# Start of a three-block kernel: the identity and the first norm's vector in transfers of their own, two weight slabs between the tiles of x, the first dense tile between the turns

## The reference, cut to what matters

```
h = rms_norm(x, attn_pre_g[l])          # x * rsqrt(mean(x*x) + eps) * g
proj = h @ w_in[l]                      # [512,1024] @ [1024,3080]
qa, ka, va, qb, kb, vb, f_logit = split(proj)
qa, ka = partial_rotary(qa, cos, sin), partial_rotary(ka, cos, sin)
lam = exp(sum(lam_q1*lam_k1)) - exp(sum(lam_q2*lam_k2)) + lam_init
log_f = log_sigmoid(f_logit + forget_bias[l])
```

## Time and profile before

| what | value |
|---|---|
| median of 3 runs | 2214.27 us (2210.42 to 2216.82) |
| profiled execution | 2209.98 us, its span 2208.7 us |
| PE busy | 2110.6 us, 96% of the span |
| DVE, ACT, POOL busy | 982.4, 814.2, 229.2 us |
| first slice of 40 (55 us): PE, DVE, ACT, POOL | 7, 6, 4, 2 tenths |
| DMA | 192.10 MB, mean 87 GB/s |

### The profile page before, as it was taken

The page is one execution under the profiler, slowest core; times in us unless marked ns, Lnnn a source line. Parts: engine busy times, 40 slices in busy tenths (PEclk is TensorE's granted clock), DMA queues, the critical chain, the costliest instruction groups (busy, mean ns, idle before and its releaser), DMA issues. The chain is left out here.

```text
span 2208.7 us, 25477 instructions
## 1 busy us (share of the span) xinstructions
PE 2110.6 (96%) x10364; PEld 1699.1 (77%) x10364; DVE 982.4 (44%) x1809; ACT 814.2 (37%) x1550; POOL 229.2 (10%) x263
## 2 busy tenths in 40 slices
PE   7999999999998999999999998999889999999997
PEld 6767688888887767688888887878655788888886
DVE  6364453323336364453333346645466444333333
ACT  4255442222224355452222324353266334222222
POOL 2004410000000004210000000000166001000000
PEclk9999999999999999999999999999999999999999
DMA  5433323233332312223333232322511233323331
GB/s 145 120 62 81 82 87 96 91 100 98 98 91 68 95 48 77 67 86 96 99 93 99 88 99 67 96 58 77 115 38 36 76 114 91 97 91 100 96 98 65
DMA packets 273833, 192.10 MB, mean 87 GB/s; under 512 B 22172, under 2 KB 241476, under 8 KB 273716
## 3 DMA queue, kind: packets, MB, share of 16 engines
q1 hardware_dynamic: 268704, 177.76, 27.9%
q0 software_dynamic: 4864, 12.67, 2.4%
q10 hardware_dynamic: 148, 0.04, 0.0%
HBM read 186.21 MB, written 4.23 MB: 86 GB/s over the span
## 5 line engine op out<-in xcount | busy, mean ns | idle before, releaser
L613 PE MATMUL bank<-h_features,weights_hi_lo 128*128 128x512 f32 (+1 forms) x5160 | 1132.8, 380 | 12.9 <-POOL h_features L1936 7.8
L613 PEld LDWEIGHTS bank<-h_features,weights_hi_lo 128*128 128x128 f32 x5160 | 930.1, 189 | 199.5 <-issue 14.8
L955 DVE TENSOR_TENSOR weights_hi_lo<-weights,weights_hi_lo 128x1024 fp32r<-128x1024 f32 (+1 forms) x337 | 400.6, 1192 | 681.7 <-ACT weights_hi_lo L1556 681.2
L1556 ACT ACTIVATE weights_hi_lo<-weights 128x1024 fp32r<-128x1024 f32 (+1 forms) x337 | 341.2, 1016 | 373.1 <-PE bank L655 350.1
L653 PE MATMUL bank<-weights_hi_lo,hidden 128*128 128x512 f32 x528 | 205.4, 389 | 0.0
L654 PE MATMUL bank<-weights_hi_lo,hidden 128*128 128x512 f32 x528 | 205.4, 389 | 0.0
L655 PE MATMUL bank<-weights_hi_lo,hidden 128*128 128x512 f32 x528 | 205.4, 389 | 0.0
L1669 ACT ACTIVATE hidden<-arena 128x512 fp32r<-128x512 f32 x66 | 41.7, 632 | 300.1 <-DVE arena L1103 300.1
L1964 POOL TENSOR_SCALAR arena<-arena,row_stats 128x256 f32<-128x256 f32 (+5 forms) x140 | 127.1, 919 | 159.8 <-DVE row_stats L1032 60.8
L1936 POOL TENSOR_TENSOR h_features<-arena,h_features 128x512 fp32r<-128x512 f32 x24 | 30.7, 1278 | 982.2 <-ACT h_features L1584 982.2
L1103 DVE TENSOR_TENSOR arena<-bank,arena 128x512 f32<-128x512 f32 x66 | 45.6, 692 | 181.3 <-PE bank L613 181.3
(11 more groups left out here) (335 smaller groups left out, 2045.7 us busy)
## 6 DMA issues: line engine op xcount, KB each, us to landing
weights<-in_w_in_dram SPq DMA_DIRECT2D x84, 512.0 KB, 3.9
weights<-in_w_gate_dram SPq DMA_DIRECT2D x66, 512.0 KB, 3.8
weights<-in_w_up_dram SPq DMA_DIRECT2D x66, 512.0 KB, 3.8
weights<-in_w_down_dram SPq DMA_DIRECT2D x60, 512.0 KB, 3.6
weights<-in_w_out_dram SPq DMA_DIRECT2D x24, 512.0 KB, 3.7
bias_rows<-decay_scratch POOLq DMA_DIRECT2D x16, 256.0 KB, 4.6
weights<-in_w_cmp_dram SPq DMA_DIRECT2D x16, 256.0 KB, 4.5
weights<-in_w_down_dram SPq DMA_DIRECT2D x12, 256.0 KB, 2.6
```

Of the source, the lines that this page charges most:

```text
L613: last = e.matmul(out_ap, l, r, start=(j == 0), stop=(j == len(pairs) - 1))
L955: e.tensor_tensor(pair_view(i, 1), raw_view(i), pair_view(i, 0).bitcast(F32), ALU.subtract).then_inc(done, tick(("split", i)))
L1556: e.activation(pair_view(i, 0), raw_view(i), ACT.Copy).then_inc(done, tick(("hi", i)))
```

## The change: what it does

The identity (64 KB) comes in a transfer of its own ahead of the other constants, the first norm's gains (16 rows) ahead of ScalarE's other transfers. SP issues x0, x1, slab 0, slab 1, x2, x3, slab 2, slab 3 in place of x0 to x3 and then the slabs. TensorE transposes the first gains alone, runs turns 0 and 1, begins the forget tile, runs turns 2 and 3, begins the qa tile, and transposes the other vectors behind it (both transposes in one bank). VectorE and ScalarE follow that order; VectorE's copies of the other vectors and the two bf16 casts come behind the split of slab 2. The functions `scaled_turn`, `low_turn`, `high_turn` are the bodies of the old loops; the other norms are as they were.

```diff
+        FIRST_GAINS = VECTOR_ROWS.pop(0)
...  tensor_program: turn(s, t) is the body of turn_norm's loop
                 def vectors():
-                    pe.wait_ge(consts_in, 32)
                     pe.wait_ge(vectors_in, VECTORS_BY_POOL)
                     pe.wait_ge(vectors_by_scalar_in, VECTORS_BY_SCALAR)
-                    e.transpose(bank("columns")[:, 0:NVEC], ROWS[0:NVEC, :], CST[0:NVEC, 0:NVEC]).then_inc(done, tick("columns"))
-                    e.transpose(bank("positions")[:, 0:64], PER[0:64, :], CST[0:64, 0:64]).then_inc(done, tick("positions"))
-
-                turn_norm("L0 attn", [("L0", "forget"), ("L0", "qk", C_QA)], vectors)
+                    out_ap = bank("columns")
+                    e.transpose(out_ap[:, 0:NVEC], ROWS[0:NVEC, :], CST[0:NVEC, 0:NVEC])
+                    e.transpose(out_ap[:, 128:192], PER[0:64, :], CST[0:64, 0:64]).then_inc(done, tick("columns"))
+
+                pe.wait_ge(identity_in, 16)
+                pe.wait_ge(first_gains_in, 16)
+                e.transpose(bank("first gains")[:, 0:16], ROWS[0:16, :], CST[0:16, 0:16]).then_inc(done, tick("first gains"))
+                turn("L0 attn", 0)
+                turn("L0 attn", 1)
+                pe.wait_ge(dve.done, dve["L0 attn", "lo", 1, 0])
+                pe.wait_ge(pool.done, pool["L0 attn", "lo", 1, 4])
+                begin_tile(("L0", "forget"), HT)
+                turn("L0 attn", 2)
+                turn("L0 attn", 3)
+                begin_tile(("L0", "qk", C_QA), HT)
+                vectors()
+                pe.wait_ge(dve.done, dve["L0 attn", "lo", 3, 0])
+                pe.wait_ge(pool.done, pool["L0 attn", "lo", 3, 4])
+                pe.wait_ge(consts_in, 32)
                 out_ap = bank("buckets")
...  vector_program
-                dve.wait_ge(consts_in, 32)
-                e.tensor_copy(IDB[:, :], IDENT).then_inc(done, tick())
-                e.tensor_copy(MKB[:, :], MASK).then_inc(done, tick("bf16"))
-                for t in range(NT - 1):
-                    diag("L0 attn", t)
-                e.tensor_copy(VC[:, :], full("columns")[:, 0:NVEC]).then_inc(done, tick("columns"))
+                e.tensor_copy(VC[:, 0:16], full("first gains")[:, 0:16]).then_inc(done, tick("first gains"))
+                banks.leave(dve, "first gains")
+                dve.wait_ge(identity_in, 16)
+                settle()
+                diag("L0 attn", 0)
+                diag("L0 attn", 1)
+                for t in range(2):
+                    scaled_turn("L0 attn", VEC["attn_pre"], t)
+                    low_turn("L0 attn", t)
+                splits(SLAB_AT["L0", "forget"] + 1)
+                diag("L0 attn", 2)
+                diag("L0 attn", 3)
+                scaled_turn("L0 attn", VEC["attn_pre"], 2)
+                splits(SLAB_AT["L0", "forget"] + 2)
+                low_turn("L0 attn", 2)
+                scaled_turn("L0 attn", VEC["attn_pre"], 3)
+                low_turn("L0 attn", 3)
+                splits(SLAB_AT["L0", "forget"] + 3)
+                e.tensor_copy(VC[:, 16:NVEC], full("columns")[:, 16:NVEC]).then_inc(done, tick("columns"))
+                e.tensor_copy(PEC[:, :], banks["columns"][:, 128:192]).then_inc(done, tick("positions"))
                 banks.leave(dve, "columns")
-                e.tensor_copy(PEC[:, :], full("positions")[:, 0:64]).then_inc(done, tick("positions"))
-                banks.leave(dve, "positions")
...
-                diag("L0 attn", NT - 1)
-                settle()
-                turned_norm("L0 attn", VEC["attn_pre"], ("L0", "forget"), False)
+                dve.wait_ge(consts_in, 32)
+                e.tensor_copy(IDB[:, :], IDENT).then_inc(done, tick())
+                e.tensor_copy(MKB[:, :], MASK).then_inc(done, tick("bf16"))
...  scalar_program
+                r, n, cols, src = FIRST_GAINS
+                e.dma_start(ARENA[r:r + n, cols[0]:cols[1]], src).then_inc(first_gains_in, 16)
+                tables()
                 for r, n, cols, src in VECTOR_ROWS[0::2]:
                     e.dma_start(ARENA[r:r + n, cols[0]:cols[1]], src).then_inc(vectors_by_scalar_in, 16)
-                tables()
-                for t in range(NT):
+                act.wait_ge(dve.done, dve["eps"])
+                def first_norm(t):
                     act.wait_ge(x_in[t], 16)
-                    act.wait_ge(dve.done, dve["eps"])
                     row_norm("L0 attn", t)
-                act.wait_ge(dve.done, dve["vectors"])
-                turned_norm("L0 attn", ("L0", "forget"))
+                first_norm(0)
+                first_norm(1)
+                high_turn("L0 attn", 0)
+                splits(SLAB_AT["L0", "forget"] + 1)
+                high_turn("L0 attn", 1)
+                first_norm(2)
+                splits(SLAB_AT["L0", "forget"] + 2)
+                first_norm(3)
+                high_turn("L0 attn", 2)
+                high_turn("L0 attn", 3)
+                splits(SLAB_AT["L0", "forget"] + 3)
...  gpsimd_program
-                e.dma_start(CST[:, :], a["shape_constants"][:, 0:NCONST]).then_inc(consts_in, 16)
+                e.dma_start(CST[:, 0:P], a["shape_constants"][:, 0:P]).then_inc(identity_in, 16)
+                e.dma_start(CST[:, P:NCONST], a["shape_constants"][:, P:NCONST]).then_inc(consts_in, 16)
...  sync_program
-                for t in range(NT):
-                    e.dma_start(X[:, t, :], a["x"][0, t * P:(t + 1) * P, :]).then_inc(x_in[t], 16)
                 for i, (_, kt, width, split, pieces) in enumerate(plan):
+                    if i in (0, 2):
+                        for t in (i, i + 1):
+                            e.dma_start(X[:, t, :], a["x"][0, t * P:(t + 1) * P, :]).then_inc(x_in[t], 16)
```

More of the change, by code:

```diff
@@ L246, in program @@
         x_in = [sem(f"x{t}_arrival") for t in range(NT)]
+        identity_in, first_gains_in = sem("identity_arrival"), sem("first_gains_arrival")
         consts_in, positions_in, vectors_in, vectors_by_scalar_in, rows_in, late_in, gain_in = (
@@ L658, in token_tiles, with turn, turn_norm @@
                                                              *([("used", i)] if t == NT - 1 else [])))
-                def turn_norm(s, begin, between=None):
-                    for t in range(NT):
[L663 to L671, removed]
+                def turn(s, t):
+                    for k0 in (0, 4):
+                        out_ap = bank((s, "turn", t, k0))
+                        pe.wait_ge(dve.done, dve[s, "diag", t])
+                        for k in range(4):
+                            last = e.matmul(out_ap[:, k * P:(k + 1) * P], X[:, t, (k0 + k) * P:(k0 + k + 1) * P], DIAG[:, t, :],
+                                            start=True, stop=True)
+                        last.then_inc(done, tick((s, "turn", t, k0)))
+                def turn_norm(s, begin):
+                    for t in range(NT):
+                        turn(s, t)
                     pe.wait_ge(dve.done, dve[s, "lo", 1, 0])
@@ L977, in gain_columns, with scaled_turn @@
                     return VC[:, at:at + 4].unsqueeze(2).to_broadcast([P, 4, P])
-                def turned_norm(s, gain, first, late):
+                def scaled_turn(s, gain, t):
+                    for k0 in (0, 4):
+                        tmp4 = turn_slot((s, t, k0))
+                        bank = full((s, "turn", t, k0))
+                        e.tensor_tensor(tmp4, bank[:, :].rearrange("p (k n) -> p k n", k=4),
+                                        VC[:, gain + k0:gain + k0 + 4].unsqueeze(2).to_broadcast([P, 4, P]), ALU.mult
+                                        ).then_inc(done, tick((s, "scaled", t, k0)))
+                        banks.leave(dve, (s, "turn", t, k0))
@@ new lines, in low_turn, with turned_norm @@
+                def low_turn(s, t):
+                    tmp4 = turns[s, t, 0].rearrange("p (k n) -> p k n", k=4)
+                    dve.wait_ge(act.done, act[s, "hi", t, 0])
+                    e.tensor_tensor(HT[:, 1, 0:4, t * P:(t + 1) * P], tmp4,
+                                    HT[:, 0, 0:4, t * P:(t + 1) * P].bitcast(F32), ALU.subtract
+                                    ).then_inc(done, tick((s, "lo", t, 0)))
+                    turns.leave(dve, (s, t, 0))
+                def turned_norm(s, gain, first):
@@ L981, in turned_norm @@
                     for t in range(NT):
-                        if late and t == 1:
+                        if t == 1:
                             diag(s, NT - 1)
[L984 to L996, removed]
+                        scaled_turn(s, gain, t)
@@ L997, in turned_norm @@
+                        low_turn(s, t)
                         if t == 1:
@@ L1255, in vector_program @@
                                     diag(f"{s} ffn", t - 1)
-                    turned_norm(f"{s} ffn", VEC["ffn_pre"] + ND * layer, (s, "gate", 0), True)
+                    turned_norm(f"{s} ffn", VEC["ffn_pre"] + ND * layer, (s, "gate", 0))
```

(12 more changed lines are left out.)

## The result

The change made the kernel slower. Five runs of each: 2222.43 us median (2221.29 to 2227.85) against 2212.89 (2210.42 to 2216.82), a ratio of 1.005 with a 95% interval of 1.0037 to 1.0063, which is 8 to 14 us. The profiled execution took 2221.77 us with a span of 2220.5, 11.8 more than before the change.

A forecast was written before the change was run, and what follows sets the result against it. Only the first 46 us, up to va, could change: angles at 31.3 plus 15.2 us of waiting for ka's bank, then ka, put va 10.5 us later; added to 2212.9 this gave 2223.4 us, range 2215 to 2229.

The forecast's parts named there:

- part 5: Bank order ahead of ka: PE idles 11 us until L1188 ends, ka begins at 46.6, va 10.5 us later.
- The bank: ka now takes forget's bank 5, so TensorE holds ka until VectorE's L1188 has read the forget tile.
- The mark: Start of va, the first stage that runs without a break: from 44.36 to 54.9, 10.5 us later.
- the sum: Angles at 31.3, plus 15.2 to L1188's end, ka 46.6 to 53.6, va at 54.9, 10.5 us later.
- The clock: ka after the long idle: 1.7 us lost to half clock, on top of 5.3; bounds 0 and 2.2.
- First turn and transfers: Start of PE: turn 0 at 7.3, a gain of 1.6 us; slab 0 at 11.5, forget tile at 16.5.
- Rival (a): Slab 0 lands late, at 15.4; first dense tile at 18.9, va shifts by 13.0, 2225.9 us; chance 0.07.
- Part 1: First turn, with the identity sent ahead: begins at 7.3, gaining 1.6 us; extra issues cost some 0.5 us, hidden.
- Between the turns: Forget half tile to second halves: half tile takes 4.0 until 20.5, slab 2's lo split ends at 30.0.
- The second halves: Dense work behind buckets: starts at 30.0 against 31.07, ends about 35.3, then PE idles 11 us until ka.
- Rival (c): Early dense tile counts in full: 6.2 us earlier and 1.7 of half clock gone, 2205 us; chance 0.02.
- Rival (b): Forget's bank is free before PE reaches ka at 35.3: no measurable change, 2213 us; chance 0.13.

The follow-up runs named there:

- e1: Changed kernel with one bank skipped ahead of ka, so ka takes bank 6 in place of forget's bank 5: 2214.43 us, ratio 1.0005.
- e2: Kernel before with five banks skipped ahead of ka, so ka takes forget's bank 2, nothing else: 2223.83 us, ratio 1.0045.
- e8: e4 with VectorE's split of slab 1 moved ahead of diagonal 3, one angle step in place of four beside it: 2209.15 us, ratio 0.9985.
- e7: e6 with the copies of the other vectors and the casts moved behind the strips: 2211.15 us, ratio 0.9994.
- e4: e1 with nine of eighteen angle steps around diagonals 2 and 3, vector copies and casts behind the strips: 2210.98 us, ratio 0.999.
- e3: e1 with SP's order of before, x0 to x3 and then the slabs: 2217.05 us in one run.
- e6: Changed kernel with SP's order of before and all four turns ahead of the first dense tile: 2215.91 us in one run.

## Why the prediction was right

The loss and its size came from part 5, and e1 and e2 show it from both sides. That the time came within 1 us (2222.43 against 2223.4) is in part luck, as the second step says. The steps:

- **The bank.** As put: ka waits for the reader of forget's bank. 10.2 us by e1, 9.6 by e2.
- **The mark and the time.** va at 56.61, 12.25 later; the sum said 54.9, 10.5 later. Every term was a little short: the start of the angles at 32.21 (31.3 said, 0.9), from there to the end of L1224 15.4 (15.2), ka with the clock 7.4 (7.0 said), and some 0.15 in the handover and the rotations. On the prediction's base of 2212.9 the 12.25 would have given 2225.2. The spans of the two profiled executions differ by 11.8, but the medians by 9.5 (the interval reaches to 13.9). Executions scatter by some us behind va alone: from va to the end they took from 2161.5 (e8) to 2168.0 us (e7). This scatter gave back what the sum had too little, and that is the luck.
- **The clock.** The step took 1.7 us from the row after 3.75 us of idle and named 2.2 as the other end; ka ran 2.1 us over 5.3, and in e2 7.9 us, 2.6 over. The term was short because the row had full clock for its first microsecond, and ka had none. The sentence on the Trainium skill (TensorE: Matmul & The Clock Gate, Part 1: The HAM clock gate) gave 11.0 in all, with half rate from the first matmul. The trace agrees: the granted clock was 0.50 from 42 us on, in the idle, and under ka's first matmul at 47.77.
- **First turn and transfers.** Turn 0 at 7.32 (7.3), first bank read at 9.44 (9.4), the forget tile at 16.96 (16.5). Rival (a), the late slab, fell: slab 0 landed at 11.3 (issued 2.12, 9.2 us), as estimated; its piece of 32-byte runs took 8.4 us and was there before it, at 10.1. What came late was x2: ScalarE waited for it until 17.64, 2.5 us past the sum's 15.1, and as said the half tile hid that (turn 2 at 21.40 follows the half tile at once). Part 1 had put an extra issue on SP at 0.5 us; but in the changed kernel's trace SP stood 3.19 us at the issue of slab 1, so x2 was issued at 5.98 only, and landed 11.6 us later.
- **Between the turns.** The norm ended later than the sum: the split of slab 0 took 2.30 in place of 1.25 and lo 2 took 1.78 in place of 0.69, both beside GpSimd's lo. This term was not in the prediction at all; lo 2 alone is 1.1 us, and the start of the angles was 0.9 late. The half tile took 4.6 us, not 4.0, and turn 2 began at 21.40, not 20.5.
- **The second halves.** 31.23, not 30.0, and for 3.4 us at half clock (7.51 us for 48 matmuls); hidden behind the bank's wait. It ended at 38.7, not 35.3, so the idle ahead of ka was 9.0 us and not 11; the end of the wait did not move by it. Rival (c) asked for 7.9 us from the early dense tile. With the bank mended and the angles away (e4) va is at 45.39, 1.0 behind the kernel before, and with the split ahead as well (e8) at 43.12, 1.2 ahead of it.
- **Rival (b)** fell with the 9.04 us of idle that L1224 ended, and with e2: the order of the banks, as read from the program, decides.

## What to carry to other kernels

Where buffers are dealt in turn, a change of the order of uses changes who waits for whom many steps later: write down, for each use, whose reader it waits for and when that reader runs, before moving anything. An early start of one tile is worth only what the end of the stage gains, so look at what starts the next unbroken stretch, not at what starts first. And in a list that is worked in order, a wait for one transfer holds all that stands behind it: e3's late slab cost its 3.3 us of waiting and more.

## What the runs showed of the hardware that was not expected

VectorE and GpSimd held each other up where both worked on SBUF alone: a split of 1.22 us took 2.30 beside GpSimd's lo (1.26), a lo of 0.69 took 1.78, a diagonal of 0.29 took 1.30; and where VectorE began first, GpSimd was the one to wait (e8: the split 1.22, GpSimd 2.11):

```profile
14.93 1.22 DVE L977 TENSOR_TENSOR weights_hi_lo<-weights,weights_hi_lo 128x1024 fp32r<-128x1024 f32 x1
15.15 2.11 POOL L2017 TENSOR_TENSOR h_features<-arena,h_features 128x512 fp32r<-128x512 f32 x1 [1.12 <-ACT h_features L1647]
```

The multiplies that read a PSUM bank keep their 0.64 to 0.69 beside it. The Trainium skill (SBUF — State Buffer, SBUF: two separate sides) describes the port pair that the two share as an exclusive lock, held by whoever starts first for a whole instruction. Among the VectorE instructions that need it, it names those with two SBUF inputs, against a GpSimd one that reads SBUF. The splits, the lo halves and GpSimd's work are of this kind, and the traces agree, by these numbers. The diagonal has one tensor as its input; that it waited too is measured, and why, no run here shows.

PE's clock fell to 0.50 at about 31.3 us in the changed kernel, after 1.5 us of idle and a product of 32 rows by 8 columns of weights, and stayed there for 3.4 us; in e8, where that idle was gone and the same product stood there, it stayed at 1.00. The other profiles go with this: before the change, in e6 and in e7 there is no idle ahead of the product, and the 72 matmuls behind it take 11.48, 11.48 and 11.49 us; in e1, e3 and e4, with 1.5 us of idle, they take 12.76, 12.97 and 12.97.

The granted clock in the windows does not tell all at the start of an execution. In the changed kernel it reads 1.00 from 8 us on, but PE ran 6 or 7 of the turns' matmuls in each of the windows from 8 to 10, and 12 of the same in the one from 11 to 12.
